# A chunked delta rule beside dense projections: the next level waits for the first update alone, and a chunk's first products are issued ahead of the state before it

## The chip, the cores and the metric

The kernel runs on one core of a Trainium2 chip. The metric is the device time of one execution in microseconds. Matmuls run on TensorE (PE in the profile; PEld is its weight load), elementwise work on VectorE (DVE) and ScalarE (ACT), the splitting of weights on GpSimd (POOL), and SyncE (SP) issues the weights' loads. Each engine runs its own list of instructions in order, and the engines meet only at semaphores.

## The reference, cut to what matters

The program is a hybrid layer with five branches (delta rule, convolution, windowed attention, gated recurrence, cross attention) and then a two-layer block; 1024 positions of 1024 channels, all in float32. The change touches the branch A alone, a gated delta rule with four heads of 128 channels. The kernel computes it in eight chunks of 128 positions. Per head and chunk, with keys k, queries q, values v, gates beta and a running sum g of log decays:

```
A_ij = beta_j * (k_i . k_j) * exp(g_j - g_i)    for i < j, else 0    (kept transposed)
U    = (I + A)^-1                               by levels: blocks of 1, 2, 4, ... 64 rows are joined
new  = U^T (beta v)  -  (decayed, beta-scaled keys through U) * S
out  = exp(g) q . S  +  (masked, decayed q.k) * new
S    = S * exp(g_last)  +  (decayed k)^T new    (the state that the next chunk starts from)
```

## The kernel before, in words

**Threads and due times.** The program is a list of sections. In each there are threads, `dense` (projections with streamed weights), `aux` (the branches' own work) and for a while `side`. A thread is a row of stages, each with a planned duration; inside a stage, every `yield` gives a fraction of it. `play` (L2452) walks the threads for each engine and always takes the piece that is due first by plan. So the planned durations decide only in which order the pieces of the two threads stand in each engine's list; the real time is set by the waits. A section's lists end before those of the next begin.

**The stretch of the change.** In the second half of the first big section, `aux` holds eight stages "A chunk n" of `CHUNK_TIME` = 70 planned us, each with a stage "A chunk n state" of 2. What lies ahead of the chunks in `aux` is planned with 294.5 us, so `aux` ends at 294.5 + 8 x 72 = 870.5. The `dense` thread of that section (A project, B glu, three memory key/value projections, C q, C k v, D x, E q, all but the first written away to DRAM) ends at 786.9 by plan, in the seventh of the eight chunks. Its pieces are two k tiles each: six matmuls of 512 columns (L343), or of 256 in the memory projections (L356). A dense half is evicted by ACT (L1048, L1155) and stored by a DMA that ACT issues (L1025); before a stage that stores, and at the stage "stored" which ends the thread, ACT waits until all stores have landed (`room`, L1028).

**A chunk.** `f_pe` first makes the transposes of k and v (L1324, L1325) and 16 products in float32 (L1321; a float32 product of 128 columns is two matmuls in the trace), and signals once. From them ACT and DVE make exponentials, the masked matrix AT and the first level's mask BT, and ACT the scaled copies VB, KBE, KDEC (L1376 to L1378). Then come the transposes of BT (L1334) and six levels. In a level PE multiplies BT and TT into bank 2, ACT copies it to ZZ (L1383), PE makes from it four products into bank 3 (for T) and four into bank 4 (for U), DVE masks the next BT (L1416) and subtracts bank 3 from TT (L1420) and bank 4 from UU (L1421). The pair of subtractions signals once, at its end, and the next level's products wait for that signal. After the levels come the state's products (L1347, L1351, L1353) and the outputs (L1359, L1360). The state stage copies the output (ACT, L1428) and updates ST (DVE, L1435). Every stage without `ahead` waits on every engine for the stages in front of it in its thread (`stage_done`, L2445), so a chunk's first transposes wait for both halves of the state stage.

**After the section**, `aux` goes on with a norm over the outputs (L615 on ACT, L630 on PE), and `dense` with "A z".

## Time and profile before

| | |
|---|---|
| median of 3 runs | 3900.77 us (3900.38 to 3906.94) |
| the profiled execution's own time | 3904.89 us |
| its span, first to last instruction | 3903.0 us |
| mean granted TensorE clock | 0.949 of full |
| PE busy in the span | 3478.7 us (89%) |
| the eight chunks, from L1324 of the first to L630 | 304.9 to 851.3 us: 546.4 us |

The span is cut into the eight chunks: each begins where its first transpose (L1324) begins. For each cut one row gives what every engine was busy and the granted clock. What such a row doesn't show is how long the PE instructions in it take when nothing holds them; that comes from single rows of the timeline, by the distance from one start to the next.

### The profile page before, as it was taken

How to read it: one execution, taken by the hardware profiler on the slowest of the kernel's cores; microseconds unless marked ns; L12 is line 12 of the kernel's file. 1: busy time of each engine (PE TensorE's matmuls, PEld its weight loads, DVE VectorE, ACT ScalarE, POOL GpSimd, SP SyncE). 2: the span in 40 equal slices, each digit the busy share in tenths (PEclk: the TensorE clock that was granted, in tenths of full speed). 3: DMA queues.
4: the chain of work that ended last, by engine and by line, in shares of the span. 5: the costliest groups of instructions: out<-in, count | busy, mean ns of one | idle time of the engine just before them, and what ended most of it. 6: DMA issues, size and time to landing. Idle time of an engine off the chain costs nothing.

```text
span 3903.0 us, 43114 instructions
## 1 busy us (share of the span) xinstructions
PE 3478.7 (89%) x16180; PEld 2777.8 (71%) x16180; DVE 1806.0 (46%) x2344; ACT 907.2 (23%) x1689; POOL 1576.6 (40%) x2013
## 2 busy tenths in 40 slices
PE   7997999978988999979899698889859988989988
PEld 6777888867766667767677477777747766678867
DVE  5763323246794554643521646574543433222343
ACT  3232112121112442323112222222211112110021
POOL 3544832204683225534453254243314433334523
PEclk9999999979999999989899899899979999999999
DMA  3122321102122012121121110000102101111211
GB/s 111 52 70 63 108 65 55 54 6 79 54 79 73 25 28 68 38 92 41 45 87 49 57 44 28 22 28 28 29 12 81 49 27 38 46 57 36 79 38 65
DMA packets 300658, 205.30 MB, mean 53 GB/s; under 512 B 25749, under 2 KB 277657, under 8 KB 300473
## 3 DMA queue, kind: packets, MB, share of 16 engines
q1 hardware_dynamic: 271241, 132.77, 12.3%
q10 hardware_dynamic: 29232, 69.95, 4.9%
q8 instruction: 129, 2.11, 0.2%
q14 instruction: 56, 0.46, 0.0%
HBM read 173.06 MB, written 29.63 MB: 52 GB/s over the span
## 4 chain that ended last, share of the span: by engine, by line
PE 61%; DVE 15%; ACT 4%; POOL 3%; issue 2%; PEld 1%; ACTq 1%; DMA 1%; PEldq 0%; DVEq 0%; POOLq 0%
PE ps L343 45%; PE ps L1321 4%; PE ps L793 3%; DVE wrk L659 3%; POOL w_lo L2512 2%; ACT wrk L821 2%; PE ps L806 1%; POOL w_hi L2507 1%; PE ps L1692 1%; PE ps L532 1%; PE ps L2024 1%; DVE wrk L846 1%; DVE small L849 1%; PE ps L356 1%; PE ps L685 1%
## 5 line engine op out<-in xcount | busy, mean ns | idle before, releaser
L2507 POOL TENSOR_TENSOR w_hi<-w_raw,pool_one 128x256 fp32r<-128x256 f32 x1004 | 685.9, 712 | 2274.0 <-PE ps L343 2241.5
L343 PE MATMUL ps<-h_hi,w_hi 128*128 128x512 f32 x2928 | 1208.4, 413 | 92.0 <-POOL w_lo L2512 23.9
L343 PE MATMUL ps<-h_lo,w_hi 128*128 128x512 f32 x2928 | 1156.9, 395 | 0.0
L343 PE MATMUL ps<-h_hi,w_lo 128*128 128x512 f32 x2928 | 1156.2, 395 | 0.0
L2512 POOL TENSOR_TENSOR w_lo<-w_raw,w_hi 128x256 fp32r<-128x256 f32 x1004 | 891.7, 917 | 23.2
L343 PEld LDWEIGHTS ps<-h_hi,w_hi 128*128 128x128 f32 x2928 | 559.7, 191 | 270.1 <-issue 103.2
L343 PEld LDWEIGHTS ps<-h_hi,w_lo 128*128 128x128 f32 x2928 | 559.0, 191 | 121.6
L343 PEld LDWEIGHTS ps<-h_lo,w_hi 128*128 128x128 f32 x2928 | 560.8, 192 | 113.3 <-issue 9.1
L343 PE MATMUL ps<-y_hi,w_hi 128*128 128x512 f32 x704 | 290.4, 413 | 30.7 <-issue 29.9
L343 PE MATMUL ps<-y_hi,w_lo 128*128 128x512 f32 x704 | 277.7, 395 | 0.0
L343 PE MATMUL ps<-y_lo,w_hi 128*128 128x512 f32 x704 | 277.5, 394 | 0.0
L659 DVE SCALAR_TENSOR_TENSOR wrk<-wrk,cols 128x1023 f32<-128x1023 f32 (+29 forms) x144 | 211.9, 1536 | 0.9 <-DVE acc L469 0.2
L343 PEld LDWEIGHTS ps<-y_hi,w_hi 128*128 128x128 f32 x704 | 134.0, 190 | 74.6 <-issue 48.4
L1321 PE MATMUL ps<-wrk 128*128 128x128 f32 x1216 | 171.8, 293 | 16.5 <-DVE wrk L1421 7.7
L1321 PEld LDWEIGHTS ps<-wrk 128*128 128x128 f32 x1216 | 159.7, 205 | 34.3 <-DVE wrk L1421 17.3
L343 PEld LDWEIGHTS ps<-y_lo,w_hi 128*128 128x128 f32 x704 | 134.4, 191 | 29.5 <-issue 3.4
L343 PEld LDWEIGHTS ps<-y_hi,w_lo 128*128 128x128 f32 x704 | 134.0, 190 | 28.8
L473 DVE TENSOR_TENSOR wrk<-ps,wrk 128x512 f32<-128x512 f32 x64 | 44.0, 688 | 225.6 <-PE ps L343 224.9
L457 ACT ACTIVATE wrk<-ps,cols 128x512 f32<-128x512 f32 x80 | 55.1, 689 | 375.2 <-PE ps L343 333.4
L793 PE MATMUL ps<-wrk 128*128 128x128 f32 (+3 forms) x416 | 96.9, 386 | 45.3 <-ACT wrk L821 32.7
L793 PEld LDWEIGHTS ps<-wrk 128*128 128x128 f32 (+1 forms) x416 | 78.6, 230 | 64.3 <-ACT wrk L821 38.5
L491 DVE TENSOR_TENSOR acc<-acc,ps 128x512 f32<-128x512 f32 x72 | 49.5, 687 | 158.1 <-PE ps L343 157.2
(343 smaller groups left out, 3815.6 us busy)
## 6 DMA issues: line engine op xcount, KB each, us to landing
w_raw<-in_w_in SPq DMA_DIRECT2D x87, 512.0 KB
w_raw<-in_even_w_in SPq DMA_DIRECT2D x48, 512.0 KB
away<-wrk ACTq DMA_DIRECT2D x80, 256.0 KB, 2.0
wrk<-away ACTq DMA_DIRECT2D x32, 512.0 KB
w_raw<-in_odd_w_in SPq DMA_DIRECT2D x32, 512.0 KB
wrk<-in_x ACTq DMA_DIRECT2D x16, 512.0 KB, 8.2
w_raw<-in_w_br SPq DMA_DIRECT2D x32, 256.0 KB
w_raw<-in_even_w_out SPq DMA_DIRECT2D x24, 256.0 KB
```

The costliest lines, as they stand in the source:

```text
L343: mm = nc.tensor.matmul(ps[:, b, 0:n], w[:, slot, k, :], rhs(part, k, b), start=(k == 0 and q == 0), stop=(k == nk - 1 and q == 2))
L356: mm = nc.tensor.matmul(ps[:, bank, 0:MEM], w[:, t % 2, k, :], rhs(part, k), start=(k == 0 and q == 0), stop=(k == KD - 1 and q == 2))
L457: nc.scalar.activation(wt(gt, b), ps[:, b, :], ACT.Sigmoid, bias=gate_bias(i)).then_inc(dense_free[b], 1)
L473: nc.vector.tensor_tensor(wt(gt, b), ps[:, b, :], wt(gt, b), ALU.mult).then_inc(dense_free[b], 1)
L491: nc.vector.tensor_tensor(y, x, ps[:, b, :], ALU.add).then_inc(dense_free[b], 1)
L532: nc.tensor.matmul(ps[:, bank + b, 0:n], ones, wt(sq, i % 2)[:, 0:n], start=(k == 0), stop=(k == nk - 1)).then_inc(summed.sem, 1)
L659: ins = nc.vector.scalar_tensor_tensor(dsts[i][:, s:T], tiles[i][:, 0:T - s], w, dsts[i][:, s:T], ALU.mult, ALU.add)
L793: mm = nc.tensor.matmul(S[:, u, c], l, r, start=True, stop=True)
L821: ins = nc.scalar.activation(SB[:, u, lo:256], src, ACT.Exp, bias=nmx[:, u:u + 1], scale=1.0 if has_bias else scale, accum_out=den[:, u:u ...
L1321: mm = nc.tensor.matmul(four(dst)[:, h, :], lhsT(h), rhs(h), start=True, stop=True)
L2507: ins = nc.gpsimd.tensor_tensor(hi, raw, one[:, 0:2], ALU.mult)
L2512: ins = nc.gpsimd.tensor_tensor(lo, raw, hi.bitcast(F32), ALU.subtract)
```

## The change

Four edits, all in the chunks.

1. `CHUNK_TIME` is 58 instead of 70, and the fractions inside a chunk are counted in 32nds, with a level every 3 of them. `aux` then ends by plan at 294.5 + 8 x 60 = 774.5, and `dense` as before at 786.9.
2. The products into bank 3 signal on their own, and the subtraction of TT too. The next level's first products wait for TT alone; the wait for UU stands at the level's second step.
3. The first products of a chunk are reordered (decay rows, beta rows, k.k, v transposed, then k transposed into bank 2, then k.q into bank 7), and PE no longer waits for the state stage as a whole: the transposes of k wait for `gdn_state_dve`, the products into bank 7 for `gdn_state_act`.
4. The count of signals per chunk follows.

```diff
-CHUNK_TIME = 70.0
+CHUNK_TIME = 58.0
...
-    lev_at = lambda lv: (9 + 4 * (lv - 1)) / 40
+    lev_at = lambda lv: (8 + 3 * (lv - 1)) / 32
...
-            for h in range(4):
-                nc.tensor.transpose(four(2)[:, h, :], acc[:, 4 + h, c], ident)
-                nc.tensor.transpose(four(3)[:, h, :], wt(h)[:, c], ident)
             products(4, lambda h: gc_t[:, n, 4 + h:5 + h].to_broadcast([P, P]), lambda h: ident)
             products(5, lambda h: beta_t[:, n, h:h + 1].to_broadcast([P, P]), lambda h: ident)
             products(6, lambda h: acc[:, 4 + h, c], lambda h: acc[:, 4 + h, c])
+            for h in range(4):
+                nc.tensor.transpose(four(3)[:, h, :], wt(h)[:, c], ident)
+            if n > 0:
+                pe.wait_ge(gdn_state_dve.sem, gdn_state_dve.nth(n - 1))
+            for h in range(4):
+                nc.tensor.transpose(four(2)[:, h, :], acc[:, 4 + h, c], ident)
+            if n > 0:
+                pe.wait_ge(gdn_state_act.sem, gdn_state_act.nth(n - 1))
             products(7, lambda h: acc[:, 4 + h, c], lambda h: acc[:, h, c]).then_inc(gdn_pe.sem, 1)
-            yield 6 / 40
+            yield 6 / 32
...
             for lv in range(1, L):
                 yield lev_at(lv)
-                pe.wait_ge(*step_dve(3 + 2 * lv))
+                pe.wait_ge(*step_dve(5 if lv == 1 else t_new(lv - 1)))
                 products(2, lambda h: BT[:, h, :], lambda h: TT[:, h, :]).then_inc(gdn_pe.sem, 1)
-                yield lev_at(lv) + 2 / 40
+                yield lev_at(lv) + 1.3 / 32
                 pe.wait_ge(*step_act(2 + lv))
+                if lv > 1:
+                    pe.wait_ge(*step_dve(u_new(lv - 1)))
                 if lv < L - 1:
-                    products(3, lambda h: UU[:, h, :], lambda h: ZZ[:, h, :])
+                    products(3, lambda h: UU[:, h, :], lambda h: ZZ[:, h, :]).then_inc(gdn_pe.sem, 1)
                 products(4, lambda h: ZZ[:, h, :], lambda h: UU[:, h, :]).then_inc(gdn_pe.sem, 1)
...
-                yield lev_at(lv) + 3 / 40
-                dve.wait_ge(*step_pe(2 * lv + 1))
-                if lv < L - 1:
-                    nc.vector.tensor_tensor(TT, TT, four(3), ALU.subtract)
+                    yield lev_at(lv) + 1.8 / 32
+                    dve.wait_ge(*step_pe(t_of(lv)))
+                    nc.vector.tensor_tensor(TT, TT, four(3), ALU.subtract).then_inc(gdn_dve.sem, 1)
+                yield lev_at(lv) + 2.3 / 32
+                dve.wait_ge(*step_pe(u_of(lv)))
                 nc.vector.tensor_tensor(UU, UU, four(4), ALU.subtract).then_inc(gdn_dve.sem, 1)
...
-        stage(f"A chunk {n}", CHUNK_TIME, pe=f_pe, act=f_act, dve=f_dve)
+        stage(f"A chunk {n}", CHUNK_TIME, ("pe",) if n else (), pe=f_pe, act=f_act, dve=f_dve)
...
-            nc.scalar.activation(acc[:, 0:4, c], four(7), ACT.Copy)
+            nc.scalar.activation(acc[:, 0:4, c], four(7), ACT.Copy).then_inc(gdn_state_act.sem, 1)
```

**Place 1.** PE's list in the last chunk, from the transposes of BT on, before the change; each pair of rows is one step of the chunk (a product counts once here, and twice in the trace).

```order
L1334 MATMUL ps<-cst,wrk 128x128 [waits gdn_act,gdn_dve]
L1334 MATMUL ps<-cst,wrk 128x128 x3
L1321 MATMUL ps<-wrk 128x128 [waits gdn_dve]
L1321 MATMUL ps<-wrk 128x128 x3
L1321 MATMUL ps<-wrk 128x128 [waits gdn_act]
L1321 MATMUL ps<-wrk 128x128 x7
L1321 MATMUL ps<-wrk 128x128 [waits gdn_dve]
L1321 MATMUL ps<-wrk 128x128 x3
```

The same engine in the last chunk after the change, from a level's first products to those of the next; L343 are the dense thread's.

```order
L1326 MATMUL ps<-wrk 128x128 [waits gdn_dve,tiles_split]
L1326 MATMUL ps<-wrk 128x128 x3
L1326 MATMUL ps<-wrk 128x128 [waits gdn_dve,gdn_act]
L1326 MATMUL ps<-wrk 128x128 x7
L343 MATMUL ps<-h_hi,w_hi 128x512 [waits dense_free0]
L343 MATMUL ps<-h_lo,w_hi 128x512
L343 MATMUL ps<-h_hi,w_lo 128x512
L343 MATMUL ps<-h_hi,w_hi 128x512
L343 MATMUL ps<-h_lo,w_hi 128x512
L343 MATMUL ps<-h_hi,w_lo 128x512
```

Before, no dense matmul stands anywhere in the last chunk; after, 156 of them do, mostly in pieces of six between the steps, though at one level the two steps stand side by side. The dense matmuls of 512 columns (256 columns) per chunk were 90 (120), 0 (264), 42 (192), 168, 168, 162, 132, 0 and are 90 (78), 0 (216), 0 (216), 102 (66), 138, 138, 138, 156.

**Place 2.** PE's list where the second chunk begins, before: the dense thread's last rows are followed by the wait for the whole state stage.

```order
L356 MATMUL ps<-y_hi,w_lo 128x256
L1324 MATMUL ps<-cst,acc 128x128 [waits aux_dve_stage_done,aux_act_stage_done,tiles_split]
L1325 MATMUL ps<-cst,wrk 128x128
L1324 MATMUL ps<-cst,acc 128x128
```

After, at the same place:

```order
L356 MATMUL ps<-y_hi,w_lo 128x256
L1326 MATMUL ps<-cst,small 128x128 x8
L1326 MATMUL ps<-acc 128x128 x4
L1332 MATMUL ps<-cst,wrk 128x128 x4
L1336 MATMUL ps<-cst,acc 128x128 [waits gdn_state_dve]
L1336 MATMUL ps<-cst,acc 128x128 x3
L1326 MATMUL ps<-acc 128x128 [waits gdn_state_act]
L1326 MATMUL ps<-acc 128x128 x3
```

Twelve products and four transposes moved ahead of the two waits on the state.

**Place 3.** ACT's list where the section ends, before: the output's copy of the last chunk is followed by the next section's first squares (L615).

```order
L1386 ACTIVATE wrk<-ps 128x512 [waits gdn_pe]
L1428 ACTIVATE acc<-ps 128x4x128 [waits aux_dve_stage_done,aux_pe_stage_done]
L615 ACTIVATE wrk<-acc 128x512 [waits aux_dve_stage_done,aux_pe_stage_done]
L615 ACTIVATE wrk<-acc 128x512
```

After:

```order
L1398 ACTIVATE wrk<-ps 128x512 [waits gdn_pe]
L1441 ACTIVATE acc<-ps 128x4x128 [waits aux_dve_stage_done,aux_pe_stage_done]
L1048 ACTIVATE wrk<-ps,cols 128x512 [waits dense_out,away_done0]
L1025 DMA away<-wrk 128x512 [waits dense_free0]
L1048 ACTIVATE wrk<-ps,cols 128x512 [waits dense_out,away_done1]
L1025 DMA away<-wrk 128x512 [waits dense_free1]
L615 ACTIVATE wrk<-acc 128x512 [waits away_done1,away_done0,dense_pe_stage_done,aux_dve_stage_done,aux_pe_stage_done]
L615 ACTIVATE wrk<-acc 128x512
```

The dense thread's last two evictions and stores now stand behind the last chunk, and the first squares wait until both stores have landed. From L615 on the lists of all engines are the same in both kernels.

## Rows read from the trace of the kernel before

**Rows 1.** The page: busy us, share of the span and count of each engine.

```profile
PE 3478.7 (89%) x16180; PEld 2777.8 (71%) x16180; DVE 1806.0 (46%) x2344; ACT 907.2 (23%) x1689; POOL 1576.6 (40%) x2013
```

**Rows 2.** Windows, a row per chunk: length, busy us by engine (count), clock, DMA.

```profile
304.90:377.50 72.60, 65.97 (x422) 59.33 (x422) 18.66 (x35) 16.95 (x40) 30.70 (x49) 0.92 0.19 59
377.50:446.00 68.50, 62.13 (x492) 59.98 (x492) 20.40 (x35) 15.25 (x46) 56.65 (x86) 0.95 0.34 101
446.00:512.50 66.50, 60.92 (x462) 57.04 (x463) 20.45 (x35) 13.88 (x43) 51.85 (x76) 1.00 0.40 108
512.50:583.30 70.80, 66.96 (x398) 57.62 (x397) 19.72 (x35) 14.22 (x31) 21.98 (x32) 0.98 0.16 51
583.30:650.20 66.90, 65.51 (x398) 56.56 (x396) 19.48 (x35) 14.12 (x31) 15.73 (x24) 1.00 0.19 58
650.20:715.90 65.70, 64.29 (x391) 55.36 (x390) 19.65 (x35) 14.12 (x31) 22.50 (x32) 1.00 0.17 53
715.90:783.30 67.40, 59.51 (x361) 51.39 (x359) 19.26 (x35) 13.54 (x30) 16.10 (x24) 0.97 0.18 55
783.30:851.30 68.00, 44.90 (x229) 40.66 (x229) 18.89 (x35) 10.17 (x26) 0.00 (x0) 0.67 0.00 0
sum 546.40, PE 490.20 PEld 437.96 DVE 156.51 ACT 112.25 POOL 215.52; mean PE 61.28 PEld 54.74 DVE 19.56 ACT 14.03 POOL 26.94
```

**Rows 3.** Timeline of PE inside chunks: start, us, line, operands, count, idle before.

```profile
442.14 0.28 PE L356 MATMUL ps<-y_lo,w_hi 128*128 128x256 f32 x1
442.26 0.28 PE L356 MATMUL ps<-y_hi,w_lo 128*128 128x256 f32 x1
...
673.63 0.39 PE L343 MATMUL ps<-h_lo,w_hi 128*128 128x512 f32 x1
673.85 0.39 PE L343 MATMUL ps<-h_hi,w_lo 128*128 128x512 f32 x1
674.08 1.95 PE L1321 MATMUL ps<-wrk 128*128 128x128 f32 x16
675.78 0.48 PE L343 MATMUL ps<-h_hi,w_hi 128*128 128x512 f32 x1
```

**Rows 4.** Waits of PE and PEld in the chunks: us in total, times, longest.

```profile
PE ps L1334 <- ACT wrk L1378: 24.5, 8, 6.3
...
PEld ps L1321 <- DVE wrk L1421: 17.3, 30, 1.7
```

**Rows 5.** Timeline of PE in the last chunk.

```profile
783.35 0.30 PE L1324 MATMUL ps<-cst,acc 128*128 128x128 f32 x1 [1.35 <-DVEq L2450]
...
794.25 1.09 PE L1334 MATMUL ps<-cst,wrk 128*128 128x128 f32 x4 [6.27 <-ACT wrk L1378]
...
820.49 1.16 PE L1321 MATMUL ps<-wrk 128*128 128x128 f32 x8 [1.38 <-DVE wrk L1421]
822.34 3.67 PE L1321 MATMUL ps<-wrk 128*128 128x128 f32 x16 [0.69 <-ACT wrk L1383]
```

**Rows 6.** GpSimd, 377.5 to 512.5: a group, count, busy, mean ns, idle, releaser.

```profile
L2507 POOL TENSOR_TENSOR w_hi<-w_raw,pool_one 128x256 fp32r<-128x256 f32 x80 | 48.1, 632 | 13.6 <-PE ps L356 13.5
```

**Rows 7.** GpSimd, one tile undisturbed, one slow: timeline.

```profile
377.48 2.33 POOL L2507 TENSOR_TENSOR w_hi<-w_raw,pool_one 128x256 fp32r<-128x256 f32 x4
379.88 2.78 POOL L2512 TENSOR_TENSOR w_lo<-w_raw,w_hi 128x256 fp32r<-128x256 f32 x4
...
454.03 2.85 POOL L2507 TENSOR_TENSOR w_hi<-w_raw,pool_one 128x256 fp32r<-128x256 f32 x4
456.96 3.58 POOL L2512 TENSOR_TENSOR w_lo<-w_raw,w_hi 128x256 fp32r<-128x256 f32 x4
```

**Rows 8.** Tile "away": the stores, from issue to landing.

```profile
DMA to landing us min/median/max: 1.9/2.0/5.7
```

**Rows 9.** Timeline: an eviction on ACT; the next section's first PE row.

```profile
643.33 0.69 ACT L1048 ACTIVATE wrk<-ps,cols 128x512 f32<-128x512 f32 x1 [5.36 <-PE ps L343]
...
851.30 1.10 PE L630 MATMUL ps<-wrk,cst 128*128 128x512 f32 x2 [2.08 <-ACT wrk L615]
```

More of the change, by code:

```diff
@@ L1303, in all4 @@
         return m.unsqueeze(1).to_broadcast([P, 4, P])
-    NPE, NACT, NDVE = 2 + 2 * NLEVEL, 3 + NLEVEL, 4 + 2 * NLEVEL
+    NPE, NACT, NDVE = 3 * NLEVEL, 3 + NLEVEL, 2 + 3 * NLEVEL
+    gdn_state_act, gdn_state_dve = sig.take("gdn_state_act", 8), sig.take("gdn_state_dve", 8)
     gdn_pe = sig.take("gdn_pe", 8 * NPE)
@@ L1309, in _hybrid @@
     L = NLEVEL
-    lev_at = lambda lv: (9 + 4 * (lv - 1)) / 40
+    lev_at = lambda lv: (8 + 3 * (lv - 1)) / 32
+    first_of, t_of = (lambda lv: 2 + 3 * (lv - 1)), (lambda lv: 3 + 3 * (lv - 1))
+    u_of = lambda lv: 4 + 3 * (lv - 1) if lv < L - 1 else 3 + 3 * (lv - 1)
+    masked, t_new = (lambda lv: 3 + 3 * lv), (lambda lv: 4 + 3 * lv)
+    u_new = lambda lv: 5 + 3 * lv if lv < L - 1 else 3 + 3 * lv
     def delta_chunk(n):
@@ L1354, in f_pe @@
             mm.then_inc(gdn_pe.sem, 1)
-            yield 37 / 40
-            pe.wait_ge(*step_dve(3 + 2 * L))
+            yield 30 / 32
+            pe.wait_ge(*step_dve(u_new(L - 1) + 1))
             for h in range(4):
@@ L1363, in f_act @@
         def f_act(act):
-            yield 2 / 40
+            yield 2 / 32
             act.wait_ge(*step_pe(0))
@@ L1367, in f_act @@
             nc.scalar.activation(eg, gc_t[:, n, 4:8], ACT.Exp).then_inc(gdn_act.sem, 1)
-            yield 4 / 40
+            yield 4 / 32
             act.wait_ge(*step_dve(0))
@@ L1372, in f_act @@
             act.wait_ge(*step_act(1))
-            yield 5 / 40
+            yield 5 / 32
             act.wait_ge(*step_dve(1))
@@ L1380, in f_act @@
             for lv in range(1, L):
-                yield lev_at(lv) + 1 / 40
-                act.wait_ge(*step_pe(2 * lv))
+                yield lev_at(lv) + 0.7 / 32
+                act.wait_ge(*step_pe(first_of(lv)))
                 nc.scalar.activation(ZZ, four(2), ACT.Copy).then_inc(gdn_act.sem, 1)
-            yield 34 / 40
-            act.wait_ge(*step_pe(2 * L))
+            yield 27 / 32
+            act.wait_ge(*step_pe(u_of(L - 1) + 1))
             nc.scalar.activation(ZZ, four(6), ACT.Copy).then_inc(gdn_act.sem, 1)
@@ L1389, in f_dve @@
             ch = chains["dve"]
-            yield 3 / 40
+            yield 3 / 32
             dve.wait_ge(*step_pe(0))
@@ L1399, in f_dve @@
             ch.link(nc.vector.tensor_tensor(acc[:, 0:4, c], acc[:, 0:4, c], EG, ALU.mult))
-            yield 5 / 40
+            yield 5 / 32
             dve.wait_ge(*step_act(1))
@@ L1407, in f_dve @@
             ch.link(nc.vector.tensor_tensor(UU, all4(ident), BT, ALU.subtract))
-            yield 7 / 40
+            yield 7 / 32
             dve.wait_ge(*step_pe(1))
@@ L1413, in f_dve @@
                 if lv < L - 1:
-                    yield lev_at(lv) + 1 / 40
-                    dve.wait_ge(*step_pe(2 * lv))
+                    yield lev_at(lv) + 0.8 / 32
+                    dve.wait_ge(*step_pe(first_of(lv)))
                     nc.vector.tensor_tensor(BT, AT, all4(C(f"lev{lv + 1}")), ALU.mult).then_inc(gdn_dve.sem, 1)
-                yield lev_at(lv) + 3 / 40
-                dve.wait_ge(*step_pe(2 * lv + 1))
-                if lv < L - 1:
-                    nc.vector.tensor_tensor(TT, TT, four(3), ALU.subtract)
+                    yield lev_at(lv) + 1.8 / 32
[3 more added lines that the diff above has]
+                dve.wait_ge(*step_pe(u_of(lv)))
                 nc.vector.tensor_tensor(UU, UU, four(4), ALU.subtract).then_inc(gdn_dve.sem, 1)
-            yield 36 / 40
-            dve.wait_ge(*step_pe(2 * L + 1))
+            yield 29 / 32
+            dve.wait_ge(*step_pe(u_of(L - 1) + 2))
             nc.vector.tensor_copy(TT, four(5)).then_inc(gdn_dve.sem, 1)
-        stage(f"A chunk {n}", CHUNK_TIME, pe=f_pe, act=f_act, dve=f_dve)
+        stage(f"A chunk {n}", CHUNK_TIME, ("pe",) if n else (), pe=f_pe, act=f_act, dve=f_dve)
         def s_act(act):
-            nc.scalar.activation(acc[:, 0:4, c], four(7), ACT.Copy)
+            nc.scalar.activation(acc[:, 0:4, c], four(7), ACT.Copy).then_inc(gdn_state_act.sem, 1)
         def s_dve(dve):
@@ L1432, in s_dve @@
                 if n == 0:
-                    nc.vector.tensor_copy(ST[:, h, :], four(2)[:, h, :])
+                    ins = nc.vector.tensor_copy(ST[:, h, :], four(2)[:, h, :])
                 else:
-                    nc.vector.scalar_tensor_tensor(ST[:, h, :], ST[:, h, :], EG[:, h, P - 1:P],
-                                                   four(2)[:, h, :], ALU.mult, ALU.add)
+                    ins = nc.vector.scalar_tensor_tensor(ST[:, h, :], ST[:, h, :], EG[:, h, P - 1:P],
+                                                         four(2)[:, h, :], ALU.mult, ALU.add)
+            ins.then_inc(gdn_state_dve.sem, 1)
         stage(f"A chunk {n} state", 2.0, act=s_act, dve=s_dve)
```

6 lines of the change are left out of this document (3 added, 3 removed).

## The prediction

> **What bounds the kernel now.** I read the page's totals first: PE is busy 89% of the span, DVE 46%, POOL 40% [rows 1], so a change is worth what it takes out of PE's waiting, its slow clock or its work. This change alters no PE work, only order and waits, so I looked at the eight chunks alone, cut where each begins [rows 2]. In six of them PE is busy for 60 to 67 of 66 to 73 us. In the last it is busy for 44.9 of 68.0 us, GpSimd does nothing, and the granted clock averages 0.67: the dense thread is out of work and the chunk's chain of dependent steps runs alone, partly at 1.2 GHz. The next to last has 59.5 busy of 67.4, since its end is bare as well.
>
> To turn this into a ledger I need the time that the same instructions take when nothing holds them. At full clock a dense matmul of 512 columns starts 0.22 to 0.23 us after the one before (I take 0.2275), one of 256 columns 0.12, and sixteen matmuls of 128 columns take 1.70 us plus about 0.09 of switching to dense, so 0.11 each [rows 3]. The stretch holds 762, 576 and 1,808 of these in both kernels: 173.4 + 69.1 + 198.9 = 441.4 us. It took 546.4 [rows 2]. The excess is 105.0 us, and only that can change. By chunk, with the counts that stand at place 1 (a chunk's own matmuls are 23.3 us in the first, 25.1 in the others), pure work is 58.2, 56.8, 57.7, 63.3, 63.3, 62.0, 55.1, 25.1; against the eight lengths of [rows 2] the excess is 14.4, 11.7, 8.8, 7.5, 3.6, 3.7, 12.3 and 42.9.
>
> **Part 1, the due times.** With 58 for 70, the same dense work is spread over all eight chunks (place 1). The last one then carries 35.5 us of dense work and has the excess of a covered chunk. What is that? The two chunks with steady 512-column cover have 3.6 and 3.7 now. Against them the new order has a thinner cover, 31.4 us of dense work per chunk in place of 38, so I go through the gaps. The head: PE waits for ACT's copies before the transposes of BT, 24.5 us in eight times, 6.27 of it in the bare last chunk [rows 4, 5], so 2.6 on average with cover. Between first products and transposes there stood 5.5 us of dense work in the covered chunks with 512 columns; the new order has again 5.5 there, so nothing changes. In a level, first products to second step: bare, the eight matmuls started at 820.49 and the sixteen at 822.34 [rows 5], so 1.85 us must pass; 0.88 are the eight themselves, and a piece of six 512-column matmuls (1.37) covers the other 0.97. Where the cover is six of 256 columns (0.72), 0.25 is left bare; this happens some three times a chunk in the second and third chunk. In each of the last five chunks one level has no piece at this place: 0.97 each. Cost: 1.0 per chunk, nearly everywhere.
>
> So I put the excess of chunks 5 to 8 at 3.6 + 1.0 - 0.5 (part 2) + 0.4 (margin for the thinner cover in the head), 4.5 each, 18 in all against 62.5 now. That is the main term: 44.5 gained. Bounds: at best 3.0 each (50.5 gained), at worst what the bare chunk shows on each of its six levels, 0.69 + 1.38 [rows 5], 12.4 more each, which eats all of it.
>
> **Part 2, the next level waits for TT alone.** Bare, the first products wait 1.38 us for the two subtractions after the four-by-four products [rows 5]. The new wait needs one subtraction (half of the 1.38), and four products (0.88) are queued between its operands and the waiting step, so it is gone even without cover. With cover most is hidden already: PEld waited 17.3 us for L1421 in 30 cases [rows 4], the longest 1.7, so the last chunk's five full ones are some 8. The other 9 us in seven chunks are 1.3 each, and a weight load's wait is partly hidden by the matmul in front of it, so I take 0.5 per chunk in chunks 1 to 7, 3.5 in all (2 of it is in the 18 above, 1.5 in the other chunks). Bounds: 0 and 9. UU's wait moves to the level's second step; UU's subtraction ends about 0.7 us after TT's and the first products plus a piece stand between, so it costs nothing. If no piece stands there it still ends before ZZ, which needs 1.85 us.
>
> **Part 3, first products beside the state.** The bare last chunk began with a wait of 1.35 us behind the state stage [rows 5]; in the others 2.7 to 4.1 us of dense work stand there, more than that wait. So it gains about 1.35 us, already inside the 42.9, and little elsewhere. New waits on the two state signals have 2.6 us of products in front of them: zero. Bounds: 0 to 2 us.
>
> **The first four chunks.** Chunk 1 keeps its head (two loads of ACT's tables and a stretch at the lower clock, 0.92 on average [rows 2]): 14. Chunks 2 and 3 are full of memory projections, whose weights GpSimd must split: 80 first-half splits, four to a tile, in 135 us are one tile per 6.75 us, and GpSimd waited 13.5 us in them for PE to free a tile [rows 6]. A tile needs 5.2 us of splitting undisturbed [rows 7]. The new order asks nine tiles per chunk in place of eleven and eight. One more cost: in chunk 2 a store is now issued in the middle of the head and ACT waits for its landing, 2.0 us by the median [rows 8], some 1.5 of it uncovered. I take 11 and 8.5, and 5.5 for chunk 4: 39.0 in all against 42.4, a gain of 3.4 (bounds -30, see rival B, and +12).
>
> **The seam, a cost.** Today the last stores have landed long before the section ends. In the new list the last two evictions and stores come after the last chunk, and L615 waits for both to land (place 3). The queue behind it on ACT is the norm, and PE's L630 waits for that. From the dense thread's last matmul: 0.3 us, the eviction 0.69, 2.0 us from issue to landing and some tenths for the issue, one square 0.6, so PE stands some 4 us [rows 8, 9]; today's wait before L630 is 2.08 and sits in the 42.9. I book 4.5 (bounds 3.5 and 8, the latter with the longest landing, 5.7).
>
> **Sum.** New excess: 39.0 + 18 + 4.5 = 61.5; 105.0 - 61.5 = 43.5 us gained, 546.4 to 503. From L615 on every list is the same, and the waits there are between engines that all start earlier together. A wait there could change only if one engine started earlier by more than another; DVE, ACT and PE all start behind the same seam. The profiled execution took 3904.89, 1.9 more than its span and 4.1 above the median. So 3861 for a profiled one and 3900.8 - 43.5 = 3857 for the median.
>
> **Rivals.**
>
> A. *The covered chunks close up better.* If chunks 4 to 8 come down to 3.0 to 3.5, chunks 2 and 3 to 7 each and chunk 1 to 13, the excess is 13 + 14 + 17 + 4.5 = 48.5 and the median 3844. For: two chunks do stand at 3.6 today. Against: the cover is thinner. Chance 15%.
>
> B. *GpSimd becomes the bound of the memory projections.* A disturbed tile took 6.5 us instead of 5.2 [rows 7]; with the 13.5 us of waiting for a free tile laid on half of the 20 tiles, 1.4 each, that is 8 us, and 24 tiles 192 us, where my ledger gives those tiles about 162. That is 30 us back: 3887. For: POOL is busy 108.5 of 135 us there [rows 2]. Against: my ledger asks one tile per 6.8 us, no faster than today's 6.75. Chance 12%. The Trainium skill, "GPSIMD Engine Reference", section 1 and key points, says that GpSimd shares its SBUF interfaces with VectorE and contends with its instructions of two SBUF inputs. That speaks against this change, which packs the same DVE work into shorter chunks; the trace agrees in kind, since tiles there took between 5.2 and 6.5 us. By the rule the share of slow tiles would rise with the share of DVE's busy time, from 0.30 to about 0.34, which is 1 or 2 us.
>
> C. *The clock.* Slower than before. A mean of 0.67 means that the lower level was granted for two thirds of the bare chunk's time, and the mean is 0.92 to 0.98 in four others [rows 2]; it followed PE's long waits. The loss is (1 - clock) times the length: 5.8 + 3.4 + 1.4 + 2.0 = 12.6 us in chunks 1 to 7 and 22 in the last. If the thinner cover let PE pause more often, every chunk could fall. The gain is eaten when the loss over the new 503 us exceeds about 56 us, a mean clock under 0.89; at 0.85 the loss is 75 in place of 12.6 and the time 3857 + 62 = 3919. Against: with dense pieces at nearly every step, waits over 2 us remain only in the heads. Chance 4%. The Trainium skill, "TensorE: Matmul & The Clock Gate", section "What's actually happening", has the slow clock as the default which activity lifts; by that rule the filled last chunk keeps the fast clock, and C needs idleness that the list doesn't show.
>
> D. *The order doesn't do it.* The pieces stand in the last chunk by the list, so only a stage behind could give the gain back: 3900, 2%.
>
> **How the numbers follow.** The main case has 67%, with its own range of 3848 to 3870; A 15, B 12, C 4, D 2. The range for 8 in 10 takes in most of A and half the way to B: 3842 to 3878. About 0.2% (8 us) is what a measurement of this kernel can tell from no change: faster 0.94, same 0.02, slower 0.04.
>
> **What would show it.** In the new trace: the last chunk at 63 to 67 us with a clock near 1; chunks 5 to 7 near 61 (56.5 + 4.5); chunks 2 and 3 at 62 and 60 with GpSimd at one tile per 6.8 us; no waits of PE or PEld for L1421's successor worth naming, and new short ones for ZZ; 4 us of PE idle before L630, whose start moves from 851 to about 808. I am wrong if chunks 5 to 8 show more than 8 us of excess each (cover), if memory tiles take 8 us (B), if the clock is under 0.9 in covered chunks (C), or if waits behind L630 grow.

## The result, and the profile after

The changed kernel took 3872.56 us by the median (3866.71 to 3876.50, 4 runs), and the kernel before, on the same chip, 3903.86. The ratio is 0.9916, with a 95% interval of 0.9899 to 0.9933: 33 us faster (26 to 39), where 43.5 were forecast. The same kernel in another set of runs took 3870.44, ratio 0.9911 (0.9892 to 0.9930). The forecast of 3857 was 15.6 us too low, inside its range. The mechanism held and its size was off. Five single executions of 5,700 to 12,100 us, in four of the versions below and in one set of the kernel before, are left out of all ratios; left out of the medians too, they would shift none by more than 1.3 us.

The profiled execution took 3866.71 us (span 3864.9), where 3861 was forecast. It was the fastest of the four. The 15.6 us that the median missed have three parts. The stretch of the chunks missed 7.6. The kernel before took 3.1 more here than in the runs that the forecast starts from (3903.86 and 3900.77). The other 5 stand in no row. Behind the stretch, from L630 to the end of the span, the profiled execution took 3049.3 us; the kernel before took 3051.7 there, a second profile of the changed kernel 3052.8, and the versions below 3048.8 to 3057.7. A few us of any whole time are therefore no matter of the chunks. The page's totals against [rows 1], engines busy:

```profile
PE 3456.1 (89%) x16180; PEld 2765.3 (72%) x16180; DVE 1810.3 (47%) x2344; ACT 906.5 (23%) x1689; POOL 1575.2 (41%) x2013
```

The count of PE's instructions is the same. The windows by chunk, cut where each chunk's first products begin (L1326 with operands cst, small), with the columns of [rows 2]:

```profile
305.00:370.30 65.30, 59.60 (x380) 54.10 (x381) 19.60 (x35) 16.05 (x36) 21.41 (x33) 0.91 0.13 41
370.30:433.70 63.40, 55.43 (x446) 53.35 (x446) 19.57 (x35) 14.70 (x43) 48.32 (x74) 0.97 0.34 100
433.70:499.90 66.20, 58.29 (x446) 57.00 (x446) 20.69 (x35) 13.31 (x42) 48.12 (x72) 0.90 0.32 95
499.90:564.50 64.60, 59.69 (x398) 54.26 (x397) 20.32 (x35) 13.39 (x34) 29.48 (x43) 0.97 0.25 64
564.50:624.70 60.20, 58.30 (x367) 51.21 (x366) 19.55 (x35) 12.73 (x29) 14.18 (x22) 1.00 0.17 53
624.70:684.80 60.10, 58.29 (x367) 51.19 (x367) 19.37 (x35) 13.20 (x30) 15.87 (x24) 1.00 0.18 53
684.80:745.60 60.80, 58.25 (x367) 51.18 (x367) 20.20 (x35) 13.53 (x30) 17.14 (x24) 1.00 0.17 53
745.60:815.60 70.00, 62.41 (x386) 54.53 (x384) 20.54 (x35) 14.73 (x33) 19.84 (x30) 1.00 0.16 49
sum 510.60, PE 470.27 PEld 426.82 DVE 159.84 ACT 111.64 POOL 214.36; mean PE 58.78 PEld 53.35 DVE 19.98 ACT 13.96 POOL 26.79
```

The stretch is 510.6 us in place of 546.4. The reader is to see two things. The last chunk has PE busy for 62.4 of 70.0 us at full clock, where [rows 2] had 44.9 of 68.0 at 0.67. And chunk 3 has the lowest clock, 0.90, where it had 1.00.

The ledger of the prediction, with the same pure work of 441.4 us (by chunk now 53.1, 51.0, 51.0, 56.2, 56.5, 56.5, 56.5, 60.6 from the new list):

| excess over pure work, us | 1 | 2 | 3 | 4 | 5 | 6 | 7 | 8 | sum |
|---|---|---|---|---|---|---|---|---|---|
| before | 14.4 | 11.7 | 8.8 | 7.5 | 3.6 | 3.7 | 12.3 | 42.9 | 105.0 |
| forecast | 14 | 11 | 8.5 | 5.5 | 4.5 | 4.5 | 4.5 | 9.0 | 61.5 |
| measured | 12.2 | 12.4 | 15.2 | 8.4 | 3.7 | 3.6 | 4.3 | 9.4 | 69.2 |

Chunk 8 holds the seam, 4.5 forecast and 3.9 measured, and keeps 5.5 beside it. Of the 7.7 us missed, chunks 3 and 4 carry 9.6, chunk 2 another 1.4; the others came out slightly better. What PE waited for in the stretch (total, times, longest), against [rows 4]:

```profile
PE ps L1344 <- ACT wrk L1390: 12.0, 5, 4.8
PE ps L1326 <- ACTq L2464: 9.6, 1, 9.6
PE ps L1344 <- POOL w_lo L2526: 7.5, 2, 3.8
PE ps L1326 <- ACT wrk L1395: 6.9, 6, 3.5
PE ps L630 <- ACT wrk L615: 3.9, 1, 3.9
PE ps L1344 <- DVE wrk L1417: 2.6, 1, 2.6
```

L1344 is the old L1334 (transposes of BT), L1326 the old L1321 (products), L1395 the old L1383 (ZZ). Nothing waits any longer for the subtractions of TT or UU. New are transposes that wait for a low half of a weight tile (w_lo), which they don't read, and one long wait of 3.5 us for ZZ. ACT's own waits for a landing; none of these lines, L615 included, reads or writes the tile that is being stored:

```profile
ACT acc L1441 <- DMA away<-wrk: 6.9, 1, 6.9
ACT wrk L1395 <- DMA away<-wrk: 5.3, 1, 5.3
ACT small L1382 <- DMA away<-wrk: 3.0, 1, 3.0
ACT wrk L615 <- DMA away<-wrk: 2.3, 1, 2.3
```

Such waits are not new. The trace of the kernel before has three in its chunks, and neither the rows nor the prediction show them:

```profile
ACT wrk L1383 <- DMA away<-wrk: 5.5, 1, 5.5
ACT acc L1428 <- DMA away<-wrk: 3.6, 1, 3.6
ACT wrk L1386 <- DMA away<-wrk: 2.9, 1, 2.9
```

The first is the same wait of ZZ's copy in chunk 3 (its copy starts at 476.37), and PE had enough dense work there to stand 1.45 us in all (to 477.94, at its end for a split). The last is in chunk 7, where PE stood 3.10 us.

In the changed kernel the one in chunk 3 explains the wait of 3.5 us. Timeline of ACT, ACT's queue and PE there:

```profile
462.25 0.93 ACTq L1025 DMA_DIRECT2D away<-wrk  x2
462.85 1.05 PE L1326 MATMUL ps<-wrk 128*128 128x128 f32 x8
467.48 0.60 ACT L1395 ACTIVATE wrk<-ps 128x512 f32<-128x512 f32 x1 [5.31 <-DMA away<-wrk]
468.13 3.79 PE L1326 MATMUL ps<-wrk 128*128 128x128 f32 x16 [3.51 <-ACT wrk L1395]
```

A level's products start at 462.85. ACT could copy them at about 463.9, but in its list the start of the next memory projection (`room`, which waits until the last two stores have landed) stands ahead of the copy. The copy comes 3.6 us late, and the sixteen products behind it take 3.79 us, which is the lower of the two clock levels (1.95 at the higher, [rows 3]). GpSimd in chunks 2 and 3, against [rows 6]:

```profile
L2526 POOL TENSOR_TENSOR w_lo<-w_raw,w_hi 128x256 fp32r<-128x256 f32 x72 | 52.2, 756 | 1.4
L2521 POOL TENSOR_TENSOR w_hi<-w_raw,pool_one 128x256 fp32r<-128x256 f32 x73 | 45.1, 648 | 32.1 <-PE ps L356 32.1
```

It waited 32.1 us for PE to free a tile, in place of 13.5, which speaks against the splitting as the bound. The seam, against [rows 9]:

```profile
815.64 1.19 PE L630 MATMUL ps<-wrk,cst 128*128 128x512 f32 x1 [3.87 <-ACT wrk L615]
```

### The profile page after: what moved, and what is told of

Its sections match the earlier page's. It is cut to its first block, busy times and chain, and to the rows that moved or that the text cites. A ratio compares the mean times of both kernels' runs of the same rounds, so it can differ in the third digit from the quotient of the medians.

```text
span 3864.9 us, 43142 instructions
## 1 busy us (share of the span) xinstructions
PE 3456.1 (89%) x16180; PEld 2765.3 (72%) x16180; DVE 1810.3 (47%) x2344; ACT 906.5 (23%) x1689; POOL 1575.2 (41%) x2013
## 3 DMA queue, kind: packets, MB, share of 16 engines
q1 hardware_dynamic: 271241, 132.77, 12.4%
## 4 chain that ended last, share of the span: by engine, by line
PE 67%; DVE 18%; ACT 5%; POOL 3%; issue 2%; ACTq 1%; PEld 1%; DMA 1%; PEldq 0%; DVEq 0%; POOLq 0%
PE ps L343 49%; PE ps L1326 4%; PE ps L793 3%; DVE wrk L659 3%; DVE wrk L638 2%; POOL w_lo L2526 2%; ACT wrk L821 2%; PE ps L806 1%; PE ps L356 1%; POOL w_hi L2521 1%; PE ps L532 1%; PE ps L1706 1%; PE ps L2038 1%; DVE wrk L846 1%; DVE small L849 1%
## 5 line engine op out<-in xcount | busy, mean ns | idle before, releaser
L343 PE MATMUL ps<-h_hi,w_hi 128*128 128x512 f32 x2928 | 1207.9, 413 | 92.3 <-POOL w_lo L2526 24.0
L343 PE MATMUL ps<-h_lo,w_hi 128*128 128x512 f32 x2928 | 1155.5, 395 | 0.0
L343 PE MATMUL ps<-h_hi,w_lo 128*128 128x512 f32 x2928 | 1155.5, 395 | 0.0
L343 PEld LDWEIGHTS ps<-h_hi,w_hi 128*128 128x128 f32 x2928 | 559.0, 191 | 269.8 <-issue 103.4
L343 PEld LDWEIGHTS ps<-h_hi,w_lo 128*128 128x128 f32 x2928 | 558.2, 191 | 121.6
L343 PEld LDWEIGHTS ps<-h_lo,w_hi 128*128 128x128 f32 x2928 | 559.9, 191 | 112.6 <-issue 9.2
L343 PE MATMUL ps<-y_hi,w_hi 128*128 128x512 f32 x704 | 290.9, 413 | 30.8 <-issue 30.0
L343 PE MATMUL ps<-y_hi,w_lo 128*128 128x512 f32 x704 | 278.2, 395 | 0.0
L343 PE MATMUL ps<-y_lo,w_hi 128*128 128x512 f32 x704 | 277.8, 395 | 0.0
L343 PEld LDWEIGHTS ps<-y_hi,w_hi 128*128 128x128 f32 x704 | 134.4, 191 | 74.8 <-issue 48.6
L1326 PE MATMUL ps<-wrk 128*128 128x128 f32 x1216 | 159.4, 280 | 9.1 <-ACT wrk L1395 6.9
L1326 PEld LDWEIGHTS ps<-wrk 128*128 128x128 f32 x1216 | 152.5, 195 | 19.8 <-ACT wrk L1395 9.4
L343 PEld LDWEIGHTS ps<-y_lo,w_hi 128*128 128x128 f32 x704 | 134.6, 191 | 29.6 <-issue 3.4
L343 PEld LDWEIGHTS ps<-y_hi,w_lo 128*128 128x128 f32 x704 | 134.1, 191 | 28.9
```

Source lines behind the costliest of these rows:

```text
L343: mm = nc.tensor.matmul(ps[:, b, 0:n], w[:, slot, k, :], rhs(part, k, b), start=(k == 0 and q == 0), stop=(k == nk - 1 and q == 2))
L1326: mm = nc.tensor.matmul(four(dst)[:, h, :], lhsT(h), rhs(h), start=True, stop=True)
```

## The experiments

All are given against the kernel before, run beside them on the same chip (medians 3908.79 for the first four, 3907.24 for the next four, 3908.81 for the last four); the stretch is that of the windows, 546.4 before and 510.6 after. "Changed" is the changed kernel. Each stretch is of one profiled execution.

| version | median us | ratio (95%) | stretch |
|---|---|---|---|
| due times only | 3879.2 | 0.9916 (0.9899 to 0.9933) | 514.3 |
| all but the due times | 3878.06 | 0.9920 (0.9904 to 0.9935) | 518.6 |
| changed, level waits for both | 3875.16 | 0.9908 (0.9893 to 0.9924) | no usable profile |
| changed, state waited for | 3871.35 | 0.9894 (0.9874 to 0.9913) | 509.6 |
| changed, again | 3870.44 | 0.9911 (0.9892 to 0.9930) | 511.5 |
| split awaited at its use | 3869.67 | 0.9906 (0.9887 to 0.9925) | 505.0 |
| landing awaited at its use | 3864.19 | 0.9893 (0.9875 to 0.9911) | 502.9 |
| "stored" moved past the seam | 3875.89 | 0.9920 (0.9900 to 0.9940) | 508.0 |
| both moved, memory only | 3861.05 | 0.9888 (0.9865 to 0.9910) | 498.0 |
| both moved, 60 per chunk | 3847.42 | 0.9851 (0.9832 to 0.9871) | 486.9 |
| changed, quarter of w_lo | 3859.64 | 0.9880 (0.9857 to 0.9902) | 497.4 |
| 70 per chunk, waits for both | 3885.86 | 0.9950 (0.9932 to 0.9967) | 524.0 |

**Which edit carries the gain?** The kernel before with the new due times alone:

```diff
-CHUNK_TIME = 70.0
+CHUNK_TIME = 58.0
```

> The kernel before with the chunk's planned duration at 58 instead of 70 and nothing else: no new signals, the old order of the first products, the old fractions. Theory M (the gain is the dense work spread over the last chunk): nearly the whole gain is here, 26 to 34 us under before; the last chunk near 65 us with a clock near 1, and PE's lost time at the seam before L630 near 4 us. Rival W (the shorter waits carry it): with 58 the levels stand closer than the old waits allow, PE waits 1 us and more for both subtractions in most levels, and at most half of the gain is left, under 16 us. Rival B (GpSimd) would show as chunks 2 and 3 no shorter than 66 us here too.

29.6 us faster, of the 31 to 37 of the changed kernel. The four last chunks have an excess of 4.8, 4.7, 5.5 and 11.0 (61.3, 61.2, 62.0 and 71.6 us long, same dense work as in the changed kernel). That is 1.1 to 1.6 more in each than in the changed kernel, and the timeline shows where. In the levels of these chunks PE waits for nothing with the due times alone, and in the changed kernel 0.69 us at one level and otherwise 0.41 at most. The difference is in the head: with the old fractions 18 dense matmuls stand ahead of the transposes of BT, with the new ones 24. Chunk 6, due times alone, then changed kernel:

```profile
635.00 0.63 PE L1334 MATMUL ps<-cst,wrk 128*128 128x128 f32 x4 [2.08 <-ACT wrk L1378]
...
635.55 0.63 PE L1344 MATMUL ps<-cst,wrk 128*128 128x128 f32 x4 [0.72 <-ACT wrk L1390]
```

In chunks 5 to 8 this wait is 2.17, 2.08, 2.58 and 3.27 us with the due times alone and 0.79, 0.72, 1.22 and 2.58 in the changed kernel. So the 1.1 to 1.6 go with the fractions, which belong to edit 1 and which this run leaves out. No run has the new fractions alone. Chunks 2 and 3 took 66.3 and 64.4 us here, and PE stood 6.79 us in chunk 2's head and 3.43 us for ZZ in chunk 3: the trouble of these chunks comes with the due times, not with the waits of edits 2 and 3.

The changed kernel with the old due times:

```diff
-CHUNK_TIME = 58.0
+CHUNK_TIME = 70.0
```

> The changed kernel with the planned duration back at 70: the new signals, order and fractions stay. Theory M: the last chunk is bare again, but its chain is shorter. Per level the bare chunk saves the wait of 1.38 us, and part of the four-by-four products' time, and the clock stays low: 68 us become 57 to 62. In the covered chunks about 0.5 us each. In all 8 to 14 us under before. Rival W: the waits carry most of the gain, 20 us or more.

30.7 us faster, far more than I gave it. Rival W asked for 20 us or more here, and theory M for 26 to 34 in the run before: both numbers came in, so the two runs don't choose between them. The last chunk, still bare, took 48.5 us in place of 68.0, which is 19.5 of the 27.8 us by which the stretch became shorter. The timeline of PE there, against [rows 5]:

```profile
796.47 3.10 PE L1326 MATMUL ps<-wrk 128*128 128x128 f32 x24 [0.69 <-ACT wrk L1395]
800.25 3.10 PE L1326 MATMUL ps<-wrk 128*128 128x128 f32 x24 [0.69 <-ACT wrk L1395]
804.04 3.10 PE L1326 MATMUL ps<-wrk 128*128 128x128 f32 x24 [0.69 <-ACT wrk L1395]
```

A level comes every 3.8 us, where it came every 6.9 (820.49 to 827.39) in [rows 5]; the three levels ahead of that one came every 7.9, their first eight matmuls too at the lower clock (2.08 us). The sixteen products and the next eight stand in one row: there is one wait per level, 0.69 for ZZ. Both parts act on the same bare chunk, so 29.6 and 30.7 don't add: together they gave 31 to 37.

Which of the edits in the levels does it? The same version, with the next level waiting for both subtractions again:

```diff
-                pe.wait_ge(*step_dve(5 if lv == 1 else t_new(lv - 1)))
+                pe.wait_ge(*step_dve(5 if lv == 1 else u_new(lv - 1)))
```

> The changed kernel with the old 70 planned us per chunk, so that its last chunk is bare, and with the next level waiting for both subtractions, as before the change. It tells what the wait for the first update alone is worth in a bare chunk, where the version with that wait has a level every 3.8 us and a last chunk of 48.5 us, against 68.0 before. Theory: the wait is the main part. Without it each of the five levels is longer by the second subtraction (0.7 us) and the four products in front of it, about 1.4 us at full clock, and by the lower clock that PE's longer waits bring (24 matmuls took 4.9 us at 1.2 GHz and 2.6 at 2.4): levels of 5.2 to 7 us, the last chunk 56 to 66, the whole 8 to 18 us above the version with 70 and the single wait (3878), 3886 to 3896. Rival (the new order of the first products and the steps' new places make the gain): the last chunk stays under 52 us and the whole within 2 us of 3878.

22.9 us faster than before, and the last chunk 52.9 us: neither theory. Two levels of it:

```profile
803.49 1.16 PE L1326 MATMUL ps<-wrk 128*128 128x128 f32 x8 [0.78 <-DVE wrk L1434]
805.33 2.05 PE L1326 MATMUL ps<-wrk 128*128 128x128 f32 x16 [0.69 <-ACT wrk L1395]
808.16 1.16 PE L1326 MATMUL ps<-wrk 128*128 128x128 f32 x8 [0.78 <-DVE wrk L1434]
```

A level takes 4.67 us. The wait behind DVE is 0.78 where it was 1.38: the products into bank 3 now signal on their own, so TT's subtraction (806.53 to 807.22) runs beside the products into bank 4, which end at 807.38. And the sixteen products take 2.05 where they took 3.67. So of the 6.9 us of a level 1.6 went with the lower clock, 0.6 with the separate signal, and 0.9 more (4.67 to 3.79) with the wait for TT alone: 4.4 us over the bare chunk. The tail behind the levels shrank from 12.35 to 9.72 us in both versions, and there too the clock differs: 0.70 was granted in the tail before, 1.00 in both of these. The Trainium skill, "TensorE: Matmul & The Clock Gate", section "What's actually happening", has the slow clock as the default which activity lifts; the rows agree in that the shorter waits came with the faster clock (0.67 granted in the chunk before, 0.90 and 0.89 in these two).

The same edit with the new due times:

> The changed kernel, but a level's first products wait for UU as before, so for both subtractions; signals and order stay. Theory M: the wait is partly covered by dense pieces of 1.4 us. From the end of the four-by-four products both subtractions need 1.4 us and a piece gives 1.37, so 0.1 to 0.3 us per level, 48 levels: 4 to 10 us slower than the changed kernel in all, less where the 256-column pieces are replaced. Rival W: more than 15 us slower.

33.6 us faster, against 31 to 37 for the changed kernel: with cover the wait for TT alone can't be told from nothing in the whole time, where I had expected it to be worth 4 to 10. It agrees with the due times alone, where PE nowhere waits for a level's subtractions and its weight loads never more than 0.4 us.

Part 3, undone on PE:

```diff
-        stage(f"A chunk {n}", CHUNK_TIME, ("pe",) if n else (), pe=f_pe, act=f_act, dve=f_dve)
+        stage(f"A chunk {n}", CHUNK_TIME, (), pe=f_pe, act=f_act, dve=f_dve)
```

> The changed kernel, but PE waits for the whole state stage in front of each chunk, as before; the new order of the first products stays. Theory M: 2.0 to 4.1 us of dense work stand between the state's products and this wait, and the state stage needs some 1.4 us, so no difference over 2 us against the changed kernel. Rival S (the first products beside the state matter): 1 us per chunk or more, 8 us slower.

37.4 us faster, a stretch of 509.6: part 3 is worth nothing that shows. Chunk 3 took 64.1 us here, with the same waits for a landing and a split, and 66.2 in the changed kernel. The record has no cause for these 2 us, so that much can't be read from a single chunk.

**Why are chunks 2 to 4 longer than forecast?** Theory Q: waits of the dense thread stand in front of a chunk's steps, since its code waits ahead of a `yield` for what it needs behind it. For the control, the changed kernel again:

> The changed kernel itself, beside the next three on one chip, so that small differences can be read. Both theories: 30 to 38 us under before.

It repeated within 2.1 us, its stretch within 1, its chunk 3 within 0.2. The split of a tile awaited just ahead of its first matmul:

```diff
-                    pe.wait_ge(tiles_split, r.t0 + j + 1)
                     yield j / r.n
+                    pe.wait_ge(tiles_split, r.t0 + j + 1)
```

and the same in `dense_run`.

> The changed kernel, but PE waits for a tile's split only when the tile's own first matmul is due, instead of one piece earlier, where a chunk's step then stands behind the wait. Theory Q (the second and third chunk lose their time to waits that stand in front of chunk steps though they belong to the dense thread): the transposes of BT no longer wait 3.77 us twice for GpSimd and the state's products 1.66, chunks 2 and 3 together 3 to 6 us shorter. Rival B (GpSimd's pace bounds the memory projections): the wait only moves to the dense matmul, chunks 2 and 3 stay at 129.5 us in sum within 1.

Chunks 2 and 3 fell to 61.5 and 62.4 us and the stretch by 6.5, but the whole only by 0.8 against the changed kernel beside it. Behind the stretch its profile took 3055.9 us, 3.1 more than that kernel's. The edit in `dense_run` reaches the whole program, but it need not be the cause: the next version leaves `dense_run` as it is and took 3057.7 there. In the head of chunk 3 another wait took the place of the old one: ACT waits 5.5 us for a landing ahead of L1379. The landing of the stores awaited just ahead of the first eviction of the memory projection:

```diff
-                for b in range(2):
-                    room(act, b)
                 for j in range(r.n):
                     yield (j + 1) / r.n
+                    if j == 0:
+                        for b in range(2):
+                            room(act, b)
```

> The changed kernel, but a memory projection's eviction waits for the landing of the last stores right before its own first copy, and no longer in front of the chunk's steps on ACT. Theory Q: the 5.3 us that ZZ's copy stood behind a landing (3.5 us of PE, and a stretch of 6.8 us at the lower clock behind it) and the 3.0 us in the head of chunk 2 go: 4 to 8 us less in chunks 2 and 3. Rival B: the time is GpSimd's, so under 2 us.

6.3 us less than the changed kernel beside it; chunks 2 and 3 took 60.5 and 60.1 us. Of ACT's four waits for a landing one is left, that of L615, and of PE's for L1396 (ZZ here) only five short ones:

```profile
PE ps L1327 <- ACT wrk L1396: 3.4, 5, 0.7
...
ACT wrk L615 <- DMA away<-wrk: 2.3, 1, 2.3
```

Both edits, the split's in the memory projections alone:

> The changed kernel with two waits moved to where they are needed, in the memory projections alone: ACT waits for the landing of the last stores just ahead of its first eviction there, and PE waits for the split of a tile just ahead of that tile's first matmul, not ahead of the chunk's step that stands in between. Theory Q (chunks 2 and 3 are longer than forecast because such waits of the other thread stand in front of a chunk's steps in the lists of ACT and PE): the landing alone brought chunks 2 and 3 to 60.5 and 60.1 us; with the split wait moved too they come to 58 to 60, and the PE waits for w_lo (3.8 us left) mostly go; the stretch 500 to 502, the whole 1 to 3 us below the version with the landing alone, about 3862. Rival (the split itself is late, GpSimd is the limit there): the wait only moves from one place in PE's list to the next, chunks 2 and 3 stay at 60 and the whole stays within 1 us of 3864.

Chunks 2 and 3 took 58.6 each, the whole 3861.05, 3.1 below the landing alone by the medians, though the ratios' intervals overlap. Theory Q stands: the two chunks' excess is 7.6 each, where I had forecast 11 and 8.5 and got 12.4 and 15.2. The waits for w_lo ahead of a chunk's transposes are gone; the only ones left are those of the memory matmuls themselves, 3.4 us in three. The rival for these chunks, GpSimd as the bound, with three quarters of its low parts left out:

```diff
-            for k in range(0, nk, 2):
+            for k in range(0, 2 if memory else nk, 2):
```

> The changed kernel, but for the memory projections' tiles GpSimd makes only one of the four pieces of the low half (three quarters of the low parts are left out there; 24 tiles, each 5.2 to 6.5 us of splitting, about 2.1 us less each, 50 us of GpSimd in all). Rival B of the prediction (GpSimd bounds the memory projections): chunks 1 to 4 would shrink by a good part of these 50 us, at least 15, and the whole to 3857 or less. Theory Q: GpSimd waits for PE to free tiles (32 us in the windows of chunks 2 and 3), so only the two PE waits for w_lo go (7.5 us by the trace, of which 2 to 6 are real since DVE's and ACT's steps that follow are late by other reasons too): the whole 2 to 8 us lower, 3863 to 3869.

Some 50 us of GpSimd's work left and the time fell by 11 to 13. GpSimd waited longer for PE, over chunks 2 and 3:

```profile
L2522 POOL TENSOR_TENSOR w_hi<-w_raw,pool_one 128x256 fp32r<-128x256 f32 x73 | 46.5, 667 | 60.2 <-PE ps L356 60.2
```

By the numbers set beforehand this run does not decide: chunks 1 to 4 became 14 to 15 us shorter and the whole 3859.6, where rival B asked for at least 15 and 3857 or less, and theory Q had 2 to 8 less. Besides, ZZ's copy waited 3.0 us for the landing here instead of 5.3, so this version changed more than GpSimd's work. What decides is that GpSimd waited for PE over half of the 119 us, and that the two moved waits gave as much with all the splitting kept. GpSimd isn't the bound.

**The seam.** "stored" moved behind the next section's first stage:

> The changed kernel, but the wait for the last stores to land moves from the section's end behind the next section's first piece. Seam theory: PE's 3.87 us before L630 shrink to about 1 us, 2 to 4 us less in all. Rival: PE then waits elsewhere for the same landing, since the next eviction writes the tile that is being stored: no change.

PE's wait before L630 fell from 3.9 to 2.2 us, and the whole did not fall (3875.89 beside 3870.44, intervals overlapping). Removing the wait alone did not show in the time. The other way to it is a plan in which the dense thread ends ahead of the end of the last chunk (786.9 against 790.5), here with both waits moved too:

```diff
-CHUNK_TIME = 58.0
+CHUNK_TIME = 60.0
```

> The version with both waits moved, with 60 for 58 planned us per chunk, so that the dense thread ends 4 us before the chunks by plan and not 12 us after. My theory of the seam: the last stores have then landed before the next section's first squares, so PE's wait before its first row there is about 2 us, as in the kernel before (2.1), and not 3.9; against it the end of the last chunk is bare over its last steps, 1 to 3 us. Chunks 5 to 7 are 1 us longer (more cover in each), the last about 5 shorter. The whole within 3 us of the version with 58, 3859 to 3865. If the seam's wait were worth its full 2 us it would be 2 lower; if the bare end costs what a bare level costs in the version with 70 (1 to 2 us a level), no gain.

13.6 us below the version with 58, far outside the 3 I allowed, and the best version of all: ratio 0.9851, 61 us below the kernel before. Its last four chunks as windows:

```profile
553.80:614.20 60.40, 59.34 (x373) 52.25 (x373) 20.77 (x35) 13.23 (x30) 17.19 (x24) 1.00 0.17 53
614.20:673.00 58.80, 57.75 (x367) 51.24 (x367) 20.86 (x35) 13.34 (x30) 17.19 (x24) 1.00 0.18 54
673.00:734.50 61.50, 59.28 (x373) 52.15 (x372) 20.27 (x35) 13.23 (x30) 17.61 (x24) 1.00 0.17 52
734.50:793.90 59.40, 55.27 (x356) 48.89 (x354) 20.25 (x35) 14.01 (x32) 16.77 (x24) 1.00 0.14 46
```

and two of PE's waits in its stretch:

```profile
PE ps L1345 <- ACT wrk L1391: 12.8, 7, 3.1
...
PE ps L630 <- ACT wrk L615: 2.1, 1, 2.1
```

Against pure work of 57.9, 56.5, 57.9 and 53.8 the excess is 2.5, 2.3, 3.6 and 5.6, where it was 3.7, 3.7, 4.3 and 9.2 with 58 (the last one's seam 2.1 for 3.9). With 58, each of the last five chunks has one level at which the first products and the second step stand side by side, and PE waited 0.69 for ZZ there. With 60 the list has a piece of six matmuls between the two at every level of every chunk, and that wait is gone from PE's list. Chunk 1 gained another 3.5 us (62.3 for 65.8, clock 0.95 for 0.91). Its head has 30 dense matmuls of 512 columns ahead of the transposes of BT in place of 24, and the wait there is 3.13 us for 4.48; but the version with the due times alone has 24 there and took 63.2, so this cause is not shown. In the stretch 11.1 us went. The other 2.5 of the medians are not in the profiles, whose spans differ by 7.1 only (3855.0 and 3847.9).

## Why the prediction was right, and where its size was off

**The main term held, its parts less so.** Excess of 4.5 per chunk in chunks 5 to 8 was forecast; measured 3.7, 3.6, 4.3 and 5.5, 17.1 in place of 18. The 0.97 for a level without a piece is there: in chunk 6 the eight matmuls start at 655.97 and the sixteen at 657.71, 0.86 more than the eight need. The 0.4 for a thinner cover in the head had the wrong sign in chunks 5 and 6, where that wait fell from 1.2 to 0.8 and 0.7 us. The 0.5 for part 2 shows in no run. These two errors offset each other, which was luck. That due times alone gave 4.8 and 4.7, near 3.6 + 1.0, was luck as well: they have no level without a piece, and their extra 1 us is the head's wait. And the sign "the last chunk at 63 to 67 us" contradicted the ledger, whose 60.6 of work with 9.0 of excess is 69.6; it took 70.0.

**Part 2 was mis-sized, twice.** With cover it is worth nothing that shows; I had 0.5 for each chunk. In a bare chunk the levels' edits gave 17 us, where the prediction put the waits there at some 8: I priced the wait and left out that the clock would be higher with the shorter waits (0.67 granted in the bare chunk before, 0.89 with the levels' edits). The sum was spared that, because the due times fill the bare chunk anyway. It is also why the two halves give 30 us each and some 35 together.

**Part 3** was booked at 1.35 inside the bare chunk and is nothing with cover, as it said.

**The first four chunks are the step that failed.** They were 39.0 by forecast and are 48.2, which is more than the 7.6 that the stretch missed. I saw one landing in ACT's list ("ACT waits for its landing", 1.5 us in chunk 2), charged that one alone, and did not look for the same wait in chunk 3, though the trace before has it there (5.5 us), nor for PE's wait on the split ahead of a chunk's step. The trace has three landings, 3.0 us of ACT's idle time in chunk 2, 5.3 and 6.9 in the midst and at the end of chunk 3, and transposes behind the split in chunks 3 and 4, 3.77 us of PE's time each. Moved to their use they gave back 6.5 us (split) and 8.6 (landings) of the stretch's 511.5 when moved alone, and 13.5 together. Some 2 of these can be chunk 3's own spread. The 5.3 cost PE 3.51 us of waiting and then 1.84 more, since the sixteen products behind it took 3.79 us in place of 1.95.

**The seam**: 4.5 booked for it, 3.87 measured, by the terms I named.

**Rivals.** B (GpSimd) is refuted: it waited 32 us for PE, and taking 50 us of its work away gave nothing beyond the moved waits. The contention by the Trainium skill's "GPSIMD Engine Reference", key points, was priced at 1 or 2 us. The trace shows no such rise: the mean of a w_hi piece went from 632 to 648 ns [rows 6], but that of a w_lo piece fell from 789 to 756:

```profile
L2512 POOL TENSOR_TENSOR w_lo<-w_raw,w_hi 128x256 fp32r<-128x256 f32 x81 | 61.5, 789 | 1.6
```

C (a lower clock in covered chunks) showed in chunk 3, 0.90, and nowhere below what [rows 2] had for the others but by 0.01. A (closer covered chunks) did not come with this change, but chunks 5 and 6 of the version with 60 are at 2.5 and 2.3, below A's 3.0 to 3.5.

## What to carry to other kernels

When two threads are merged into one list per engine, look at what each wait stands in front of, not only at what it waits for: a wait issued ahead of a hand-over point holds the other thread's next step. Put it behind the hand-over, right at its use. Before pricing a saved wait in a stretch without cover, look at the clock of that stretch; the wait may be the smaller part. And where planned durations set the order, a scan of them is worth its cost: 58 and 60, both with the two waits moved, differ by 14 us here.

## What was not expected of the hardware

In the bare chunk 0.67 of the clock was granted with 2.07 us of waits in each level of 6.9 to 7.9, and 0.90 with 1.47 in each of 4.67. A single wait of 3.51 us in the midst of covered work was followed by sixteen products at half speed, 3.79 us, though PE was busy for 58.3 of that chunk's 66.2 us. The length of the wait doesn't tell it alone: behind the two waits of 3.77 us, in chunks 3 and 4 of the changed kernel, the transposes ran at the lower level once and at the higher once.

```profile
447.16 1.12 PE L1344 MATMUL ps<-cst,wrk 128*128 128x128 f32 x4 [3.77 <-POOL w_lo L2526]
...
513.34 0.66 PE L1344 MATMUL ps<-cst,wrk 128*128 128x128 f32 x4 [3.77 <-POOL w_lo L2526]
```

The landing of a store took 1.9 us at least and 6.3 at most after the change, with the median still at 2.0 [rows 8].
